# One decoder layer on Trainium2: the gate and up products of both FFNs by a seven-product block scheme

## Chip, cores and metric

One core of one Trainium2 chip runs the whole program. The metric is device time in microseconds (us) for one execution; lower is better.

## What is computed

One inference step of a decoder layer for 1024 prompt tokens and 64 sample tokens, 1088 together, with width 1024 and FFN width 2816, in fp32:

```python
x = x + 0.5 * (silu(h @ w1_gate) * (h @ w1_up)) @ w1_down     # h = rmsnorm(x), first FFN
z = rmsnorm(x) @ w_in                                         # mLSTM q,k,v,i,f,o; attention q,k,v; two gates
y_m = mlstm(z) @ w_up_m
y_a = dilated_attention(z) @ w_up_a
x = x + (sigmoid(gm) * y_m + sigmoid(ga) * y_a) @ w_out
x = x + 0.5 * (silu(h @ w2_gate) * (h @ w2_up)) @ w2_down     # h = rmsnorm(x), second FFN
y = rmsnorm(x)
```

## The kernel before

Everything that is multiplied is split into two float32r parts, a rounded one (hi) and what is left (lo); a product is three matmuls, hi*hi, hi*lo and lo*hi, added in PSUM. Activations lie with features on the 128 partitions and tokens along the free axis; `x` holds [128, 8, 1088] in SBUF. Tokens are cut into three chunks of 384, 384 and 320 (`CHUNKS`).

Weights come as slabs of 128 x 2048 (1 MB) in the order of use. SP loads them into three buffers `raw` (`slab_behind`), GpSimd splits each into `whi` and `wlo` (`split`, L711 and L716, eight pieces of 256 columns each), and TensorE reads them.

An FFN is 11 passes (`step` inside `ffn` of the tensor block), each over 256 hidden columns with three slabs. Slab 1 and 2 hold the gate and up columns of 128 hidden units each. `pair_unit` (L838, L841, L842) makes for one slab and one chunk 8 k x 2 (gate, up) x 3 = 48 matmuls into two PSUM banks. Then ScalarE takes silu of the gate (L1288), VectorE multiplies by up in PSUM (L1731), ScalarE rounds (L1290) and VectorE makes the low part (L1733) into `act_hi`, `act_lo`. `down` (`products`, L811, L814, L815) multiplies slab 3 by these: per chunk eight output tiles of 6 matmuls, through four PSUM banks, and VectorE adds each with factor 0.5 to `x` (L1722). Gate, up and down of a pass stand one after the other in TensorE's order, so only 256 hidden columns exist at a time and `x` stays where it is.

The norm ahead of a product works by chunk: ScalarE squares (L1261), VectorE adds up (L1672), TensorE sums over partitions with a matrix of ones (L822), ScalarE takes the root, VectorE the reciprocal (L1678) and the scaled `htmp` (L1692), ScalarE rounds it to `h_hi` (L1278) and VectorE makes `h_lo` (L1700). At an FFN's end the next norm of chunk 0 lies beside the products of chunk 2 in the last pass.

Behind the first FFN come the value products (45 units of 24 matmuls, 256 wide, L811 with `whi` moving), the other projections (`pair_unit` again), then mLSTM and attention, then the branch products and gates (`mx_hi`, L2201 to L2207) and the output products (`OUNITS`), all in chunks. Every engine's order is written out by hand with semaphores.

## Time and profile before

| | |
|---|---|
| median of 3 runs | 2791.04 us (2786.9 to 2793.04) |
| the profiled execution | 2801.94 us, its span 2799.6 us |
| TensorE busy | 2601.7 us, 16124 matmuls |
| VectorE, ScalarE, GpSimd busy | 949.6, 392.7, 1089.1 us |
| read from memory, written | 172.83 MB, 45.89 MB |

The profiled execution is one of its own, 0.4% above the median. Matmuls are pipelined: their listed durations overlap, and the pace is the distance between starts.

### The profile page before, as it was taken

Reading aid. Unit: us, or ns where it says so; the run is one execution under the profiler, and the core shown is the slowest. Engines: PE = TensorE matmul, PEld = TensorE weight load, DVE = VectorE, ACT = ScalarE, POOL = GpSimd, SP = SyncE. Lnnn points to the kernel's source line nnn. Section 1 sums busy time; section 2 is a strip of 40 time slices with the busy share of each in tenths; the row PEclk is TensorE's granted clock in tenths of the full one; section 3 lists DMA queues with packets and bytes.
Section 4 is the critical chain, followed back from the end, with each engine's and each line's share of the span. In section 5 each row is a group of like instructions: output and inputs, shape, how many; then the busy total and the mean of one; then the engine's idle time right before and its main releaser. Section 6 shows DMA issues by size and latency. Waiting matters only on the chain. (4 is left out here: it accounts for less than half of the span.)

```text
span 2799.6 us, 41223 instructions
## 1 busy us (share of the span) xinstructions
PE 2601.7 (93%) x16124; PEld 2545.1 (91%) x16126; DVE 949.6 (34%) x1885; ACT 392.7 (14%) x823; POOL 1089.1 (39%) x1681
## 2 busy tenths in 40 slices
PE   5899999999989999999996884679899999999997
PEld 5899999999988999999995673679899999999997
DVE  6322222222256101232004575543622222222226
ACT  4100000000022011000113451112200000000003
POOL 5444444444443644343411222232544444444440
PEclk9999999999999999999997897789999999999998
DMA  4111111111101522222315638351111111111101
GB/s 156 46 46 45 45 40 36 44 45 45 45 31 61 171 103 94 93 90 95 94 48 171 210 132 294 133 177 42 46 46 45 45 45 45 45 45 45 45 0 64
DMA packets 85204, 220.24 MB, mean 79 GB/s; under 512 B 10932, under 2 KB 63596, under 8 KB 70124
## 3 DMA queue, kind: packets, MB, share of 16 engines
q1 hardware_dynamic: 60472, 189.25, 19.8%
q10 hardware_dynamic: 24628, 29.50, 3.0%
q8 instruction: 78, 1.28, 0.2%
q14 instruction: 26, 0.21, 0.0%
HBM read 172.83 MB, written 45.89 MB: 78 GB/s over the span
## 5 line engine op out<-in xcount | busy, mean ns | idle before, releaser
L838 PE MATMUL ps<-h_hi,whi 128*128 128x384 f32 (+1 forms) x3072 | 1012.5, 330 | 25.1 <-POOL wlo L716 15.8
L711 POOL TENSOR_TENSOR whi<-raw,con 128x256 fp32r<-128x256 f32 x792 | 474.2, 635 | 1414.3 <-PE ps L838 1119.3
L842 PE MATMUL ps<-h_hi,wlo 128*128 128x384 f32 (+1 forms) x3072 | 1009.2, 329 | 0.7 <-issue 0.7
L841 PE MATMUL ps<-h_lo,whi 128*128 128x384 f32 (+1 forms) x3072 | 1009.2, 329 | 0.0
L838 PEld LDWEIGHTS ps<-h_hi,whi 128*128 128x128 f32 x3072 | 578.1, 188 | 30.9 <-POOL wlo L716 17.9
L841 PEld LDWEIGHTS ps<-h_lo,whi 128*128 128x128 f32 x3072 | 578.3, 188 | 0.6
L842 PEld LDWEIGHTS ps<-h_hi,wlo 128*128 128x128 f32 x3072 | 578.1, 188 | 0.0
L716 POOL TENSOR_TENSOR wlo<-raw,whi 128x256 fp32r<-128x256 f32 x792 | 571.9, 758 | 0.0
L811 PE MATMUL ps<-act_hi,whi 128*128 128x384 f32 (+1 forms) x1056 | 348.3, 330 | 14.4 <-DVE x L1722 14.4
L1731 DVE TENSOR_TENSOR ps<-silu,ps 128x384 f32<-128x384 f32 x132 | 71.3, 540 | 833.3 <-PE ps L842 549.4
L814 PE MATMUL ps<-act_lo,whi 128*128 128x384 f32 (+1 forms) x1056 | 347.4, 329 | 0.0
L815 PE MATMUL ps<-act_hi,wlo 128*128 128x384 f32 (+1 forms) x1056 | 347.1, 329 | 0.0
L1722 DVE SCALAR_TENSOR_TENSOR x<-ps,x 128x384 f32<-128x384 f32 (+1 forms) x528 | 279.3, 533 | 183.8 <-PE ps L815 182.3
L1288 ACT ACTIVATE silu<-ps 128x384 f32<-128x384 f32 x132 | 62.5, 473 | 1260.3 <-PE ps L842 1260.3
L811 PEld LDWEIGHTS ps<-act_hi,whi 128*128 128x128 f32 x1056 | 199.6, 189 | 15.3 <-DVE x L1722 15.1
L814 PEld LDWEIGHTS ps<-act_lo,whi 128*128 128x128 f32 x1056 | 199.5, 189 | 0.3
L815 PEld LDWEIGHTS ps<-act_hi,wlo 128*128 128x128 f32 x1056 | 199.5, 189 | 0.0
L811 PE MATMUL ps<-whi,h_hi 128*128 128x256 f32 x360 | 100.8, 280 | 3.8 <-DVE x L1722 3.8
L815 PE MATMUL ps<-whi,h_lo 128*128 128x256 f32 x360 | 100.4, 279 | 0.0
L814 PE MATMUL ps<-wlo,h_hi 128*128 128x256 f32 x360 | 100.3, 279 | 0.0
L1733 DVE TENSOR_TENSOR act_lo<-ps,act_hi 128x384 fp32r<-128x384 f32 x132 | 70.7, 535 | 71.2 <-ACT act_hi L1290 71.2
L811 PE MATMUL ps<-h_hi,whi 128*128 128x384 f32 (+1 forms) x216 | 72.5, 336 | 12.7 <-POOL wlo L716 10.3
(222 smaller groups left out, 2120.0 us busy)
## 6 DMA issues: line engine op xcount, KB each, us to landing
raw<-stream SPq DMA_DIRECT2D x99, 1024.0 KB, 4.9
vc<-vc_in SPq DMA_DIRECT2D x8, 1170.0 KB, 7.8
kc<-kc_in SPq DMA_DIRECT2D x8, 1152.0 KB, 11.3
zgate<-stage ACTq DMA_DIRECT2D x16, 384.0 KB, 2.5
sgate<-zgate SPq DMA_DIRECT2D x16, 384.0 KB, 3.5
zqko<-stage ACTq DMA_DIRECT2D x12, 384.0 KB, 2.5
oc<-o_att SPq DMA_DIRECT2D x8, 396.0 KB, 6.0
va_out<-sva ACTq DMA_DIRECT2D x24, 130.0 KB, 2.0
```

Of the source, the lines that this page charges most:

```text
L711: pool.tensor_tensor(whi[:, j, cut], raw[:, j, cut], con[:, C_ONES:C_ONES + 1].to_broadcast([P, SPLIT]), ALU.mult).then_inc(hi_split, 1)
L716: low_part = pool.tensor_tensor(wlo[:, j, cut], raw[:, j, cut], whi[:, j, cut].bitcast(F32), ALU.subtract)
L811: mm = pe.matmul(out, w_hi, x_hi, start=(k == 0), stop=False)
L814: pe.matmul(out, w_hi, x_lo, start=False, stop=False)
L815: last = pe.matmul(out, w_lo, x_hi, start=False, stop=(k == nk - 1))
L838: mm = pe.matmul(out, w_hi, h_hi[:, k, a:a + w], start=(k == 0), stop=False)
L841: pe.matmul(out, w_hi, h_lo[:, k, a:a + w], start=False, stop=False)
L842: mm = pe.matmul(out, w_lo, h_hi[:, k, a:a + w], start=False, stop=(k == KT - 1))
L1288: act.activation(silu[:, j, 0:w], bank(2 * j, w), ACT.Silu).then_inc(silu_done, 1)
L1722: dve.scalar_tensor_tensor(x[:, d, a:a + w], bank(4 + v % 4, w), 0.5, x[:, d, a:a + w], ALU.mult, ALU.add).then_inc(acc_free, 1)
L1731: dve.tensor_tensor(up, silu[:, j, 0:w], up, ALU.mult).then_inc(mul_done, 1)
L1733: dve.tensor_tensor(act_lo[:, j, a:a + w], up, act_hi[:, j, a:a + w].bitcast(F32), ALU.subtract).then_inc(pair_free, 1)
```

## The change

The gate and up products become a phase of their own, ahead of all down products. Weights of a gate slab are a 2 x 2 block matrix (gate and up columns; two halves of the 1024 features), and so are the normed tokens (two halves of the features; two blocks of 272 tokens); the 8 block products of their product are made by 7, Winograd's form of Strassen's scheme. The steps:

- Tokens are cut into 2 halves of 544, each into 2 blocks of 272. VectorE's `prepare` scales `x` in place and makes the sums and differences of blocks there; ScalarE's `token_high` rounds the seven operands into `chi`, VectorE writes low parts into `clo` and into `xlo`, which lies where `x` lies. After that `x` itself is gone; it comes back from memory (`x_reload`, the input or a copy stored in `x_kept`) for the down phase.
- A slab's seven weight operands: ScalarE rounds (`gate_high`, 512 columns each), GpSimd makes low parts (`low`) and the four differences in place (`less`). Gate slabs have two buffers.
- `fast` makes for a slab and a token half seven products of 4 k x 3 matmuls, 272 wide, into four PSUM banks; two units alternate between banks 0 to 3 and 4 to 7. VectorE's nine `gate_part` steps combine them, ScalarE takes silu, and the finished 128 x 544 block goes to memory (`hidden_out`) by `gate_store`.
- The down phase loads 256 hidden columns per pass back (`load_hidden`), splits them (`hidden_high`, `hidden_low`) and multiplies as before, in chunks of 384, 384, 320.
- At the FFN's end the norm of chunk 0 begins with the second down chunk. The branch and output products go over four parts of 272 tokens instead of the three chunks. Some semaphores are merged.

```diff
+QW = 272
+PARTS = tuple((QW * i, QW) for i in range(TOK // QW))
+NP = len(PARTS)
+GU = 2 * FFN_ITERS
+FU = 2 * GU
...
+WINO = ((0, 9, 1), (1, 16, 6), (2, 17, 4), (3, 18, 5), (0, 14, 3), (1, 19, 2), (2, 10, 7))
+FSUM_BANK = (0, 4, 0, 4)
...
+        xlo = place("xlo", [P, KT, TOK], F32R, 16512)
...
+            def gate_behind(n, s, b):
+
+                sp.wait_ge(wcl_done, 7 * (s + GU * n - 1))
+                gate_slab(n, s, b)
+
+            def gate_store(n, u, s, q):
+                sp.wait_ge(wino_step, 9 * (u + FU * n) + 9)
+                sp.dma_start(hidden_out[s, :, 2 * QW * q:2 * QW * (q + 1)],
+                             gout[:].rearrange("p j t -> p (j t)")).then_inc(hidden_st, 16)
+
+            def x_reload(n, q):
+                a = slice(2 * QW * q, 2 * QW * (q + 1))
+                sp.dma_start(x[:, :, a], (xT if n == 0 else x_kept)[:, :, a]).then_inc(x_in[1 + q], 16)
+
+            def load_hidden(n, i):
+                sp.wait_ge(hidden_st, 16 * (FU * n + (FU - 2 if i < FFN_ITERS - 1 else FU)))
+                if i > 2:
+                    sp.wait_ge(actlo_done, 3 * (FFN_ITERS * n + i - 2))
+                j = (S_D[n] + i) % 3
+                sp.dma_start(hst[:, j], hidden_out[2 * i:2 * i + 2].rearrange("s p t -> p s t")).then_inc(hst_in[j], 16)
+
...
+                gate_store(n, 41, 20, 1)
+                gate_store(n, 42, 21, 0)
+                x_reload(n, 0)
+                load_hidden(n, 0)
+                gate_store(n, 43, 21, 1)
+                sp.wait_ge(wino_full, 7 * FU * (n + 1))
+                x_reload(n, 1)
+                slab(S_D[n] + 1, (S_D[n] + 1) % 3, shift)
+                load_hidden(n, 1)
+                slab(S_D[n] + 2, (S_D[n] + 2) % 3, shift)
+                for i in range(2, FFN_ITERS):
+                    s = S_D[n] + i + 1
+                    if n == 0 or s < S_D[n] + FFN_ITERS:
+                        slab_behind(s, s % 3, shift)
+                    load_hidden(n, i)
 
...
+            def gate_split(s, b):
+
+                def low(p, col, need):
+                    pool.wait_ge(wch_done, 7 * s + need)
+                    for a in range(0, 512, SPLIT):
+                        cut = slice(a, a + SPLIT)
+                        ins = pool.tensor_tensor(wcl[b][p][:, cut], raw[:, b, col + a:col + a + SPLIT],
+                                                 wch[b][p][:, cut].bitcast(F32), ALU.subtract)
+                    ins.then_inc(wcl_done, 1)
+
+                def less(out, one, two):
+                    for a in range(0, 512, SPLIT):
+                        piece = lambda col: raw[:, b, col + a:col + a + SPLIT]
+                        ins = pool.tensor_tensor(piece(out), piece(one), piece(two), ALU.subtract)
+                    ins.then_inc(wsum_done, 1)
+
+                low(0, 0, 1)
+                low(5, 1536, 2)
+                low(4, 512, 3)
+                less(0, 1024, 0)
+                less(1024, 1536, 1024)
+                pool.wait_ge(wsum_done, 4 * s + 1)
+                less(1536, 1536, 0)
+                low(2, 0, 4)
+                low(3, 1024, 5)
+                low(1, 1536, 6)
+                pool.wait_ge(wsum_done, 4 * s + 3)
+                less(512, 512, 1536)
+                low(6, 512, 7)
...
+            def half_sum_products(f):
+                for k in range(KT):
+                    pe.wait_ge(fsq_ready, 8 * f + k + 1)
+                    for i in range(2):
+                        mm = pe.matmul(bank(FSUM_BANK[f] + i, QW), ones, fsq[:, k % 2, QW * i:QW * (i + 1)],
+                                       start=(k == 0), stop=(k == KT - 1))
+                    mm.then_inc(fsq_used, 1)
+                pe.wait_ge(fsq_used, KT)
...
+            def fast(u, par, b, q, weights=None, tokens_=None, middle=None):
+
+
+                for p, (off, need_h, need_w) in enumerate(WINO):
+                    if p == 0 and not (isinstance(u, int) and u < 2):
+                        pe.wait_ge(wino_step, 9 * u - 10)
+                    if p == 4:
+                        pe.wait_ge(gate_silu, 3 * u + 1)
+                    if p > 4:
+                        pe.wait_ge(wino_step, 9 * u + (p - 4))
+                    if weights is not None:
+                        pe.wait_ge(wcl_done, 7 * weights + need_w)
+                    if tokens_ is not None:
+                        pe.wait_ge(xprep, 19 * tokens_ + need_h)
+                    out = bank(4 * par + off, QW)
+                    lo = low_half(q, p)
+                    for k in range(4):
+                        cut = slice(k * P, (k + 1) * P)
+                        pe.matmul(out, wch[b][p][:, cut], chi[q][p][:, k, :], start=(k == 0), stop=False)
+                        pe.matmul(out, wch[b][p][:, cut], lo[:, k, :], start=False, stop=False)
+                        mm = pe.matmul(out, wcl[b][p][:, cut], chi[q][p][:, k, :], start=False, stop=(k == 3))
+                    mm.then_inc(wino_full, 1)
+                    if p == 0 and middle is not None:
...
+                U, X = FU * n, GU * n
+                b0, b1 = n, 1 - n
+                if n == 0:
+                    half_sum_products(1)
+                fast(U, 0, b0, 0, X, 2 * n, (lambda: half_sum(3)) if n == 1 else None)
+                pe.wait_ge(fstd_ready, 2 * n + 2)
+                fast(U + 1, 1, b1, 0, X + 1)
...
+            def gate_high(s, b, count, kinds):
+
+                for p, col, need in kinds:
+                    if need == 0:
+                        act.wait_ge(graw_in[b], count)
+                    else:
+                        act.wait_ge(wsum_done, 4 * s + need)
+                    act.activation(wch[b][p][:], raw[:, b, col:col + 512], ACT.Copy).then_inc(wch_done, 1)
+
+            PLAIN = ((0, 0, 0), (5, 1536, 0), (4, 512, 0))
+            SUMS = ((2, 0, 1), (3, 1024, 2), (1, 1536, 3))
+            LAST = ((6, 512, 4),)
...
+                    half_square(1, 0)
+                    half_square(1, 1)
+                    token_high(0, 1)
+                    token_high(0, 2)
+                    half_square(1, 2)
+                    half_square(1, 3)
+                    token_high(0, 3)
+                    token_high(0, 4)
+                    token_high(0, 5)
+                    first_slab(0, SUMS)
+                    half_square(1, 4)
+                    half_square(1, 5)
+                    token_high(0, 6)
+                    half_square(1, 6)
+                    half_square(1, 7)
+                half_root(f1)
+                gate_silus(U, 0, 0)
+                first_slab(n, LAST)
+                gate_high(X + 1, b1, loaded + 16, PLAIN)
+                gate_silus(U, 0, 1)
+                token_high(f1, 0)
+                gate_high(X + 1, b1, loaded + 16, SUMS)
+                gate_silus(U, 0, 2)
+                gate_silus(U + 1, 1, 0)
+                token_high(f1, 1)
+                token_high(f1, 2)
+                gate_high(X + 1, b1, loaded + 16, LAST)
+                token_high(f1, 3)
...
+                def slab_time(s, count, b):
+
+
+                    gate_silus(2 * s + U, 0, 0)
+                    act.wait_ge(wino_full, 14 * s + 7 * U)
+                    gate_high(s + (X + 1), b, count, PLAIN)
+                    gate_silus(2 * s + U, 0, 1)
+                    gate_high(s + (X + 1), b, count, SUMS)
+                    gate_silus(2 * s + U, 0, 2)
+                    gate_silus(2 * s + (U + 1), 1, 0)
+                    gate_high(s + (X + 1), b, count, LAST)
+                    gate_silus(2 * s + (U + 1), 1, 1)
+                    gate_silus(2 * s + (U + 1), 1, 2)
...
+                at_ = lambda tile, part: tile[:, part[0], part[1]]
+                if m < 8:
+                    if f >= 2 and m == 0:
+                        dve.wait_ge(x_saved2[q], 16)
+                    tok = slice(2 * QW * q, 2 * QW * (q + 1))
+                    o = C_G + 16 * (f // 2) + m
+                    ins = dve.scalar_tensor_tensor(x[:, m, tok], x[:, m, tok], con[:, o:o + 1], fsum[:, q, :], ALU.mult, ALU.mult)
+                elif m in (10, 11, 12, 14):
+                    dve.wait_ge(xprep, 19 * f + (8, 8, 11, 0, 13)[m - 10])
+                    out, one, two, op = {10: (A22, A21, A22, ALU.add), 11: (A21, A11, A21, ALU.subtract),
+                                         12: (A11, A22, A11, ALU.subtract), 14: (A12, A12, A11, ALU.subtract)}[m]
+                    ins = dve.tensor_tensor(at_(x, out), at_(x, one), at_(x, two), op)
+                else:
+                    part, p, keep, need = {8: (A11, 0, 0, 1), 9: (A22, 6, 2, 2), 13: (A12, 4, 1, 3), 15: (A11, 1, None, 6),
+                                           16: (A22, 2, None, 4), 17: (A21, 3, None, 5), 18: (A12, 5, None, 7)}[m]
+                    dve.wait_ge(xhi_done, 7 * f + need)
+                    dst = at_(xlo, part) if keep is None else clo[q][keep][:]
+                    ins = dve.tensor_tensor(dst, at_(x, part), chi[q][p][:].bitcast(F32), ALU.subtract)
+                ins.then_inc(xprep, 1)
...
+            def gate_part(u, par, m):
+
+                A, B, C, E = (bank(4 * par + i, QW) for i in range(4))
+                S, U4, Y1, Y2 = gsum[:, 0, :], gsum[:, 1, :], gout[:, 0, :], gout[:, 1, :]
...
+                if m == 5 and not (isinstance(u, int) and u == 0):
+                    dve.wait_ge(hidden_st, 16 * u)
...
+                out, one, two = ((S, B, G1), (U4, C, S), (gup[:], E, U4), (S, E, S), (G1, A, G1),
+                                 (Y1, B, U4), (Y1, G1, Y1), (G2, C, S), (Y2, G2, gup[:]))[m]
+                dve.tensor_tensor(out, one, two, ALU.mult if m in (6, 8) else ALU.add).then_inc(wino_step, 1)
...
+                dve.wait_ge(x_in[1], 32 * (n + 1))
+                dve.wait_ge(x_in[2], 32 * (n + 1))
+                downs(0, (S_D[n] + 1) % 3)
...
                 for d in range(KT):
                     accumulate(i, 1, d)
                     if d > 1:
                         add_square(g1 + 1, d - 1)
+                    if d == 4:
+                        inverse(g1)
+                    if d >= 5:
+                        norm_step(g1, d - 5)
...
```

GpSimd, a gate slab. Before, the rows of one slab begin so (`whi`, `wlo`: rounded and low part):

```order
7 L719 ISA
8 L708 ISA
9 L711 ISA
10 L711 TENSOR_TENSOR whi<-raw,con 128x256 x8
11 L715 ISA
12 L716 TENSOR_TENSOR wlo<-raw,whi 128x256
```

Now, the middle of one slab (`wch`, `wcl`: rounded and low operand of a product; `raw<-raw`: a difference of weight blocks):

```order
14 L850 TENSOR_TENSOR raw<-raw 128x256 x4
15 L858 ISA
16 L850 TENSOR_TENSOR raw<-raw 128x256 x2
17 L840 REGISTER_ALU
18 L843 TENSOR_TENSOR wcl_2_110<-raw,wch_2_96 128x256 x2
19 L840 REGISTER_ALU
20 L843 TENSOR_TENSOR wcl_3_111<-raw,wch_3_97 128x256 x2
21 L840 REGISTER_ALU
22 L843 TENSOR_TENSOR wcl_1_109<-raw,wch_1_95 128x256 x2
23 L863 REGISTER_ALU
24 L850 TENSOR_TENSOR raw<-raw 128x256 x2
```

The rounding went to ScalarE; GpSimd has 22 subtractions in place of 8 products and 8 subtractions, and most follow a rounding of ScalarE's.

ScalarE, the head of the program. Before (squares of chunk 0, root, eight roundings, and only then the squares of chunk 1):

```order
1 L1261 ACT_TABLE_LOAD
2 L1261 ACTIVATE ssum<-x 128x384
3 L1261 ACTIVATE sq<-x 128x384 x7
4 L1271 ACT_TABLE_LOAD
5 L1271 ACTIVATE rstd<-ps,con 128x384
6 L1278 ACTIVATE h_hi<-htmp 128x384 x8
7 L1261 ACTIVATE ssum<-x 128x384
8 L1261 ACTIVATE sq<-x 128x384 x7
```

Now, its second part (`chi`: rounded token operands of the first half; `fsq`: squares of the second half; `fsum<-ps`: the second half's root):

```order
14 L1513 ACTIVATE chi_2_82<-x 128x1088
15 L1513 ACTIVATE chi_3_83<-x 128x1088
16 L1513 ACTIVATE chi_1_81<-x 128x1088
17 L1522 ACTIVATE wch_2_96<-raw 128x512
18 L1522 ACTIVATE wch_3_97<-raw 128x512
19 L1522 ACTIVATE wch_1_95<-raw 128x512
20 L1496 ACTIVATE fsq<-x 128x544 x2
21 L1513 ACTIVATE chi_5_85<-x 128x1088
22 L1496 ACTIVATE fsq<-x 128x544 x2
23 L1502 ACTIVATE fsum<-ps,con 128x544
```

The last squares of the second half stand behind the copy `chi_5`, and TensorE's sums over all eight squares (`half_sum_products`) stand ahead of its first product.

SP, from the gate phase to the down phase (before, SP only loads slabs there, each behind `slab_ready`):

```order
35 L510 DMA hidden_out<-gout 128x544 [waits wino_step] x2
36 L515 DMA x<-xT 128x8x544
37 L522 DMA hst<-hidden_out 128x2x1088 [waits hidden_st]
38 L510 DMA hidden_out<-gout 128x544 [waits wino_step]
39 L515 DMA x<-xT 128x8x544 [waits wino_full]
40 L493 DMA raw<-stream 128x2048
41 L522 DMA hst<-hidden_out 128x2x1088 [waits hidden_st]
42 L493 DMA raw<-stream 128x2048
```

The second half of `x` is requested when the last product of the phase has ended.

## Rows read from the trace of the kernel before

**Rows 1.** The page: span, and busy time of each engine

```profile
span 2799.6 us, 41223 instructions
PE 2601.7 (93%) x16124; PEld 2545.1 (91%) x16126; DVE 949.6 (34%) x1885; ACT 392.7 (14%) x823; POOL 1089.1 (39%) x1681
```

**Rows 2.** Stages: stretch, length, busy us (count) PE, PEld, DVE, ACT, POOL, clock, DMA, GB/s

```profile
0.00:23.90 23.90, 1.62 (x2) 0.50 (x2) 12.41 (x15) 8.68 (x14) 12.79 (x21) 1.00 0.88 324
23.90:87.50 63.60, 49.43 (x235) 46.95 (x236) 48.30 (x73) 29.21 (x52) 25.92 (x33) 0.89 0.14 50
87.50:826.30 738.80, 738.80 (x4452) 738.53 (x4451) 208.25 (x383) 66.34 (x137) 315.43 (x492) 1.00 0.12 43
826.30:847.80 21.50, 14.44 (x76) 13.77 (x74) 16.89 (x30) 11.31 (x21) 16.67 (x21) 0.84 0.27 98
847.80:992.50 144.70, 138.51 (x1156) 137.41 (x1155) 50.64 (x92) 9.73 (x21) 65.73 (x96) 0.99 0.36 117
1774.50:1866.60 92.10, 81.00 (x432) 79.40 (x432) 52.87 (x105) 15.53 (x35) 0.00 (x0) 0.89 0.56 187
1877.20:1976.20 99.00, 98.99 (x580) 98.42 (x580) 45.01 (x70) 19.81 (x39) 44.64 (x63) 0.97 0.12 43
2779.20:2799.60 20.40, 1.55 (x3) 0.50 (x2) 15.82 (x27) 2.41 (x5) 0.00 (x0) 0.62 0.39 141
```

**Rows 3.** TensorE in order of time: start, duration, matmul; first and last of three runs

```profile
299.74 0.34 PE L815 MATMUL ps<-act_hi,wlo 128*128 128x384 f32 x1
303.98 0.34 PE L815 MATMUL ps<-act_hi,wlo 128*128 128x384 f32 x1
304.68 0.31 PE L838 MATMUL ps<-h_hi,whi 128*128 128x320 f32 x1
310.84 0.31 PE L838 MATMUL ps<-h_hi,whi 128*128 128x320 f32 x1
929.78 0.28 PE L814 MATMUL ps<-wlo,h_hi 128*128 128x256 f32 x1
931.93 0.28 PE L815 MATMUL ps<-whi,h_lo 128*128 128x256 f32 x1
```

**Rows 4.** GpSimd in order of time: start, duration of eight; FFN 1, then the head

```profile
326.81 5.61 POOL L716 TENSOR_TENSOR wlo<-raw,whi 128x256 fp32r<-128x256 f32 x8
...
30.96 8.10 POOL L716 TENSOR_TENSOR wlo<-raw,whi 128x256 fp32r<-128x256 f32 x8
```

**Rows 5.** Groups by line and shape: busy us, mean ns of one, idle before

```profile
L1731 DVE TENSOR_TENSOR ps<-silu,ps 128x384 f32<-128x384 f32 x88 | 49.5, 562 | 588.7 <-PE ps L842 549.4 <-ACT silu L1288 39.4
L1278 ACT ACTIVATE h_hi<-htmp 128x384 fp32r<-128x384 f32 x48 | 25.1, 522 | 37.3 <-DVE htmp L1692 37.1
L1731 DVE TENSOR_TENSOR ps<-silu,ps 128x320 f32<-128x320 f32 x44 | 21.8, 496 | 244.5 <-ACT silu L1288 244.5
L1678 DVE RECIPROCAL rstd<-rstd 128x384 f32<-128x384 f32 x8 | 20.4, 2553 | 19.1 <-ACT rstd L1271 19.1
L1678 DVE RECIPROCAL rstd<-rstd 128x320 f32<-128x320 f32 x4 | 8.6, 2152 | 5.9 <-ACT rstd L1271 5.9
```

**Rows 6.** VectorE, SBUF to SBUF: beside GpSimd's splits, then (last two) alone

```profile
821.14 0.85 DVE L1692 SCALAR_TENSOR_TENSOR htmp<-x,con,rstd 128x384 f32<-128x384 f32 x1
821.92 0.96 DVE L1700 TENSOR_TENSOR h_lo<-htmp,h_hi 128x384 fp32r<-128x384 f32 x1
...
2766.95 0.55 DVE L1672 TENSOR_TENSOR ssum<-ssum,sq 128x384 f32<-128x384 f32 x1
...
L1692 DVE SCALAR_TENSOR_TENSOR yst<-x,con,rstd x24: 546/609/619, 2756.0 to 2796.6; 128x384 f32<-128x384 f32 x16, 128x320 f32<-128x320 f32 x8
```

**Rows 7.** A load and a store (page), and DMA by slices of 0.75 us, 0 to 30

```profile
raw<-stream SPq DMA_DIRECT2D x99, 1024.0 KB, 4.9
...
zgate<-stage ACTq DMA_DIRECT2D x16, 384.0 KB, 2.5
...
GB/s 0 0 105 197 229 371 399 377 395 476 407 426 366 363 383 379 375 374 371 361 364 364 393 409 425 415 426 448 404 306 33 0 0 109 218 426 371 273 0 0
```

875 lines of the change are left out of this document (543 added, 332 removed).

## Prediction

> **What bounds the kernel now.** I read the page's busy table first, then the table by stages, then the order of time on the single engines. TensorE is busy 2601.7 of 2799.6 us [rows 1], and the chain that ended last is made of it; but a busy share of matmuls says little, so the question is at what pace it goes where, and where it stands. The stages [rows 2] answer: the long stretch of FFN 1 (87.5 to 826.3) is without a hole, at granted clock 1.00, with VectorE at 28%, ScalarE at 9%, GpSimd at 43% and DMA at 12%. TensorE's own pace sets the end there, and only fewer or narrower matmuls help. Between them lie short stages in which norms, weight splits and loads stand in its way.
>
> That pace is read from starts of consecutive matmuls [rows 3]: 128x384 goes from 299.74 to 303.98 in 24 steps, 0.1767 us each; 128x320 from 304.68 to 310.84 in 42, 0.1467 us; 128x256 from 929.78 to 931.93 in 19, 0.1132 us. Their listed durations (about 0.3 us) are latencies and overlap. One pass over 256 hidden columns has 288 of the wide and 144 of the narrow matmuls, a third of each in the down products: 50.9 + 21.1 = 72.0 us. Eleven passes are 792 us. FFN 1 ends at 847.8, so it loses 55.8 us, 46.9 at its head (23.9 before the first product) and 8.9 at its end, where 76 matmuls, some 12.6 us, fill 21.5; FFN 2 runs from 1976.2 to 2779.2 and loses 11.
>
> **What the change removes.** A gate slab (128 gate and 128 up columns) has 144 matmuls now: 96 x 0.1767 + 48 x 0.1467 = 24.0 us. The new scheme has 2 token halves x 7 products x 4 k x 3 split terms = 168 matmuls of 272 columns. No row has that width. By the straight line from 256 to 320 one takes 0.1216 us; by the 256-wide price per column 0.1203; by the line through 320 and 384 carried down 0.1242. I take 0.122, near the first, and keep 0.120 and 0.1245. A slab is then 168 x 0.122 = 20.5 us, 3.5 less; 44 slabs give **-154 us**. At the two ends it is -169 and -136. The down products keep their 144 matmuls: 24.0 us a pass.
>
> **Does another engine set the pace of the gate phase?** Each against 20.5 us a slab.
> - GpSimd: 14 subtractions for low parts and 8 for weight differences, all 256 wide, two operands. Eight now start 5.6 us apart in all, 0.70 each [rows 4]: 22 x 0.70 = 15.4, plus about 1 us of waiting for ScalarE's rounded copies. It can begin a slab only when TensorE starts the slab before: ScalarE's first copy stands behind its read of that slab's first product, some 2.3 us in. It ends about 19 us in, so some 4 us are spare.
> - ScalarE: 7 copies 512 wide and 6 steps 272 wide; at 522 ns for 384 [rows 5], no more than 7 x 0.70 + 6 x 0.52 = 8.0 us.
> - VectorE: 18 parts 272 wide; 562 ns at 384, 496 at 320 [rows 5] make 0.45: 8.1 us.
> - PSUM: product 5 overwrites bank 0 after ScalarE copied it out (due 5.9 us in, done by 2.5), and banks change sides between units; nothing is late. Stores of 278 KB and loads of 1 MB per 20.5 us are some 80 GB/s, against 324 moved in the first 23.9 us [rows 2].
> - SP: behind its wait for a slab's last low part (about 19 us into the slab before) stands the store of that slab's second unit, due at 21; VectorE's 6th part of the next unit waits for that store, due near 29. A store of 384 KB lands after 2.5 us [rows 7], so nothing stops.
>
> So TensorE still sets the pace. GpSimd is the one with little room. Where VectorE adds or scales from SBUF to SBUF meanwhile, the same eight subtractions took 8.10 us, and VectorE's 384-wide steps 0.96 us instead of 0.55 [rows 4, 6]; beside VectorE operations with a PSUM operand they took 5.6. In the steady phase 4 of 18 parts have no PSUM operand, 1.6 us a slab, and by the rows the cost is within the spare 4 us. The Trainium skill (SBUF — State Buffer, the shared port pair) says that a VectorE operation with two SBUF inputs and a GpSimd operation exclude each other for a whole instruction, which speaks against this change; by that rule GpSimd would need 15.4 + 1.6 + 1 = 18 us here, still under 20.5, and the contended rows agree with it.
>
> **What the change adds, at the joins.**
> - Head of FFN 1. TensorE now waits for half of all tokens and, before its first product, for the square sums of the other half; ScalarE's last two squares stand behind a copy that needs VectorE's 15th preparation step. The walk: x rows land at about 10 us, adds to 16, sum and root to 18.6, reciprocal 3.6 (2553 ns at 384, 2152 at 320 [rows 5]) to 22.2, eight scalings 544 wide to 28 and seven steps 1088 wide to 37 (609 ns at 384 and 546 at 320 [rows 6] carry on to 0.76 and 1.3), copies, weight copies, squares and sums to 42. The first unit then ends at about 55, since the clock is low after idling (0.89 over the first stage after the start now [rows 2]). Slab 1's copies stand behind silu and preparation: 7 us of stall; the second half's preparation, partly at contended prices, another 6 to 9; slab 2's split can start only when the third unit has left its buffer, 2 us. Head in all about 64 instead of 46.9: **+17** (bounds +8, all preparation at free prices, to +30, all at contended ones).
> - Gate to down, twice. x was used up as combinations and comes back from memory; its second half, 2.23 MB, is requested when the last product ends. A 1 MB load lands after 4.9 us alone [rows 7], so 10.7 at that rate, 5.6 at the about 400 GB/s that the first window's best slices reach [rows 7]; I take 8. VectorE waits for it, and TensorE runs four products (4.2 us) ahead into its four banks. Stall some 6, with the clock 8: **+16** for both (8 to 30). The split of the first down slab is hidden behind the last two units.
> - End of FFN 1. The norm of chunk 0 no longer lies beside gate products of chunk 2 but inside the last 15.5 us of down products: VectorE has 2.55 of reciprocal, 16 accumulations, 16 square additions and 8 steps at about 1.9 (0.85 and 0.96 [rows 6]) there, about 31 us; chunk 1's norm slides into the value products. Together 26 us lost against 8.9 + 10.3 (144.7 us for 134.4 of products after it): **+7** (0 to 15).
> - Mixer outputs in four parts of 272: 576 + 768 matmuls at 0.122, 164 us, for 168 now. The out products take 99.0 us now [rows 2], and gain about 4; the branches (92.1 for 72 of products [rows 2]) hang on VectorE and the gate loads, 32 rounds instead of 24, and lose about 3. **-1** (-5 to 8).
> - Head of FFN 2. First slab's weight differences come after the last out product, 5 us; then the same stalls as above, about 18: 23 for 11 now. **+12** (5 to 22).
> - Tail. The last chunks' norms meet a VectorE that also accumulates; from the start of the second down chunk (now 15.5 us ahead of 2779.2 [rows 2]) the root comes at 8, the reciprocal at 10.4, chunk 1's sum at 17, the last product at 23, the last square's addition at 35, scaled outputs and stores at 45; 36 now. **+9** (5 to 12).
>
> Attention between 1473 and 1774 keeps its work. Sum: -154 + 17 + 16 + 7 - 1 + 12 + 9 = -94 against 2801.94 us, the profiled execution's own time, 0.4% over the median 2791.04. So 2707 for a profiled one and, by the same 0.4%, **2697 us** as median.
>
> **Rivals.**
> - *GpSimd sets the pace* (slower). If its 22 operations cost what eight cost beside VectorE's SBUF work, 8.10/8 = 1.01 us [rows 4], a slab takes 22 x 1.01 + 0.8 = 23.0 us, and 44 x 2.5 = 110 us come back: 2807, slower. It eats the whole gain from 0.99 us per operation on; at 0.93 the loss is 33 us (2730). For it: 15.4 of 20.5 us in use, two operands throughout, chains to ScalarE. Against: 0.70 in the steady phase [rows 4]. 12 in 100, 5 of them past the turning point.
> - *Narrow matmuls cost their columns alone*: 272 at 2.4 GHz are 0.1133 us. Then 44 x 168 x 0.0087 = 64 us more, 2633. For it: what a row adds to its columns falls with the width, 16.7 ns at 384 and 6.5 at 256 [rows 3]. Against: no row is without it. 6 in 100. The Trainium skill (TensorE: Matmul & The Clock Gate, Back-to-back issue gap) adds a fixed 2.5 ns to the columns; by that rule the result would be 2651, but every interval of this trace is longer than it gives.
> - *The joins cost all that they can*: 117 instead of 60, 2754. 10 in 100.
> - *It doesn't do what it says*: if a slab still issued 192 matmuls of 272, it would take 23.4 us and gain 27 us, less than the joins cost. The order of instructions has seven products of 12 per half; 1 in 100.
>
> **How the numbers follow.** The forecast has 71 in 100. Its own bounds: joins at their low sum of 21 and a matmul at 0.120 give 2643; joins at 117 and 0.1245 give 2772. I let the range end at 2645 and 2765, which takes in the milder GpSimd cases and leaves out the cheap matmuls and the worst corners. A measurement here tells 0.2%, 5.6 us, from no change. Faster 0.92, same 0.02, slower 0.06 (GpSimd past its turning point, and 1 for what I don't see).
>
> **What would show it.** In the new profile: gate matmuls 0.120 to 0.1245 us apart at clock 1.00; 168 per 20.5 us; GpSimd's pairs about 1.4 us with idle time before each slab; a start at about 42 us; a hole of 5 to 8 us between gate and down; some 31 us for the last two down chunks of FFN 1. TensorE waiting for low weight parts all through the gate phase, or intervals over 0.13, would prove me wrong.

## The result, and the profile after

The changed kernel takes 2781.15 us (median of 6 runs, 2771.38 to 2785.04) against 2793.14 (6 runs, 2786.9 to 2805.1): ratio 0.9943 with a 95% interval of [0.992, 0.9967] (the medians alone divide to 0.9957). It is faster, as forecast, but by some 0.5% for the forecast 3.4%; 2781 lies above the range. The profiled execution took 2771.38 us, its span 30.1 us less than before [rows 1]. It is the fastest of the six, and the profiled execution of the kernel before lies 9 us above its median, so the stages account for 30 us of gain where the medians show 12. All stage figures below are of that execution, unless a run is named. Below, a *unit* is the 84 gate products of one weight slab and one half of the tokens, two units to a slab; the *head* of an FFN is the time up to about its sixth unit, from which on TensorE hardly waits in the gate phase (the *steady run*); the *join* is where the gate phase ends and the first down pass begins; the *tail* is the end of the program.

The page of the changed kernel, the lines that answer to [rows 1]:

```profile
span 2769.5 us, 47348 instructions
PE 2514.5 (91%) x17550; PEld 2452.1 (89%) x17550; DVE 1261.0 (46%) x2482; ACT 593.7 (21%) x1165; POOL 1348.7 (49%) x1945
```

Its stages, columns as in [rows 2]: in FFN 1 the start, the head, the steady run, the join (hole and first down pass) and the last down pass; then the branch, the out products, and the head of FFN 2:

```profile
0.00:44.00 44.00, 14.14 (x37) 9.57 (x37) 27.46 (x26) 23.77 (x33) 16.59 (x24) 0.96 0.39 152
44.00:133.97 89.97, 70.26 (x504) 69.41 (x505) 51.73 (x74) 28.04 (x48) 56.25 (x69) 0.87 0.15 52
133.97:502.90 368.93, 368.93 (x2943) 368.93 (x2942) 148.14 (x315) 111.85 (x229) 276.21 (x386) 1.00 0.20 75
536.20:572.60 36.40, 27.29 (x146) 26.83 (x145) 17.49 (x30) 4.33 (x6) 19.22 (x29) 0.91 0.76 297
787.10:821.55 34.45, 28.34 (x151) 26.19 (x149) 30.25 (x54) 15.78 (x30) 13.42 (x16) 0.90 0.08 31
1745.50:1850.10 104.60, 83.93 (x575) 82.23 (x576) 58.42 (x143) 18.05 (x49) 0.00 (x0) 0.88 0.55 170
1860.80:1960.00 99.20, 99.20 (x771) 99.04 (x772) 43.30 (x63) 20.82 (x27) 33.53 (x52) 0.98 0.15 55
1960.00:2064.20 104.20, 74.85 (x512) 73.24 (x511) 57.00 (x75) 30.56 (x52) 63.52 (x85) 0.84 0.19 70
```

The third line is the phase that the change was made for: 35 units of 84 products in 368.93 us, TensorE without a hole at clock 1.00, so 368.93 / 2940 = 0.1255 us a product and 21.08 us a slab. The lines around it are where that gain went: heads at clock 0.84 to 0.87 with 22% and 28% of TensorE's time empty, a join with 27 of 36 us busy, a branch that grew from 92.1 [rows 2] to 104.6.

GpSimd in the middle of the steady run, one slab (start, duration, form, idle before), beside [rows 4]; last, eight of its subtractions in the head:

```profile
347.61 4.21 POOL L843 TENSOR_TENSOR wcl<-raw,wch 128x256 fp32r<-128x256 f32 x6 [4.55 <-ACT wch L1522]
351.77 4.42 POOL L850 TENSOR_TENSOR raw<-raw 128x256 f32<-128x256 f32 x6
356.16 4.42 POOL L843 TENSOR_TENSOR wcl<-raw,wch 128x256 fp32r<-128x256 f32 x6
360.54 1.43 POOL L850 TENSOR_TENSOR raw<-raw 128x256 f32<-128x256 f32 x2
362.70 1.43 POOL L843 TENSOR_TENSOR wcl<-raw,wch 128x256 fp32r<-128x256 f32 x2 [0.74 <-ACT wch L1522]
...
46.76 7.70 POOL L843 TENSOR_TENSOR wcl<-raw,wch 128x256 fp32r<-128x256 f32 x8 [2.12 <-ACT wch L1522]
```

From 347.61 to 364.13 it does its 22 operations, with 4.55 us idle before them: the spare 4 us of the prediction. In the head eight take 7.70 us, near the 8.10 of [rows 4].

By the prediction's own terms, in us, from the two profiled spans (a slab before is 24.0 us, a down pass 72.0 / 3):

| term | forecast | measured | how |
|---|---|---|---|
| gate slabs | -154 | -128.5 | 44 x (24.0 - 21.08) |
| head of FFN 1 | +17 | +25.4 | last gate product at 536.1, less 22 x 21.08 = 463.8, less 46.9 |
| two joins | +16 | +26.4 | hole 4.7 and first pass 31.8 for 23.8; 4.6 and 32.9 for 23.8 |
| end of FFN 1 | +7 | -1.9 | last pass 34.3, value stage 141.2 for 134.4 of products; 19.2 lost before |
| branch and out | -1 | +12.8 | 104.6 for 92.1, 99.2 for 99.0, 0.1 between |
| head of FFN 2 | +12 | +31.6 | 506.3 from the last out to the last gate product, less 463.8, less 10.9 |
| tail | +9 | +7.2 | last pass 31.5 for 23.8, 0.5 less behind it |
| rest | 0 | -3 | down passes 23.8 for 24.0; projections, attention +1 |
| sum | -94 | -30 | |

### The profile page after: what moved, and what is told of

It is laid out like the page before. It is cut to its first block and busy times, and to the rows that moved or that the text cites. A ratio compares the mean times of both kernels' runs of the same rounds, so it can differ in the third digit from the quotient of the medians.

```text
span 2769.5 us, 47348 instructions
## 1 busy us (share of the span) xinstructions
PE 2514.5 (91%) x17550; PEld 2452.1 (89%) x17550; DVE 1261.0 (46%) x2482; ACT 593.7 (21%) x1165; POOL 1348.7 (49%) x1945
## 5 line engine op out<-in xcount | busy, mean ns | idle before, releaser
L1054 PE MATMUL ps<-chi,wch 128*128 128x272 f32 x2464 | 718.9, 292 | 50.7 <-POOL wcl L843 34.0
L1056 PE MATMUL ps<-chi,wcl 128*128 128x272 f32 x2464 | 717.5, 291 | 0.0
L843 POOL TENSOR_TENSOR wcl<-raw,wch 128x256 fp32r<-128x256 f32 x616 | 450.7, 764 | 350.1 <-ACT wch L1522 350.1
L1054 PEld LDWEIGHTS ps<-chi,wch 128*128 128x128 f32 x2464 | 471.2, 191 | 53.7 <-POOL wcl L843 36.0
L1056 PEld LDWEIGHTS ps<-chi,wcl 128*128 128x128 f32 x2464 | 470.4, 191 | 0.0
L1055 PE MATMUL ps<-xlo,wch 128*128 128x272 f32 x1408 | 411.1, 292 | 0.0
L979 PE MATMUL ps<-act_hi,wsp 128*128 128x384 f32 (+1 forms) x1056 | 353.2, 334 | 23.6 <-DVE x L2132 14.8
L982 PE MATMUL ps<-act_lo,wsp 128*128 128x384 f32 (+1 forms) x1056 | 350.0, 331 | 0.0
L983 PE MATMUL ps<-act_hi,wsp 128*128 128x384 f32 (+1 forms) x1056 | 349.7, 331 | 0.0
L1006 PE MATMUL ps<-h_hi,wsp 128*128 128x384 f32 (+1 forms) x960 | 314.6, 328 | 2.9 <-issue 1.8
L1010 PE MATMUL ps<-h_hi,wsp 128*128 128x384 f32 (+1 forms) x960 | 314.2, 327 | 0.0
L979 PEld LDWEIGHTS ps<-act_hi,wsp 128*128 128x128 f32 x1056 | 201.8, 191 | 27.1 <-DVE x L2132 16.8
L983 PEld LDWEIGHTS ps<-act_hi,wsp 128*128 128x128 f32 x1056 | 201.9, 191 | 0.0
```

The costliest lines, as they stand in the source:

```text
L843: ins = pool.tensor_tensor(wcl[b][p][:, cut], raw[:, b, col + a:col + a + SPLIT], wch[b][p][:, cut].bitcast(F32), ALU.subtract)
L979: mm = pe.matmul(out, w_hi, x_hi, start=(k == 0), stop=False)
L982: pe.matmul(out, w_hi, x_lo, start=False, stop=False)
L983: last = pe.matmul(out, w_lo, x_hi, start=False, stop=(k == nk - 1))
L1006: mm = pe.matmul(out, w_hi, h_hi[:, k, a:a + w], start=(k == 0), stop=False)
L1010: mm = pe.matmul(out, w_lo, h_hi[:, k, a:a + w], start=False, stop=(k == KT - 1))
```

## Experiments

The edits are shortened to what matters; words in brackets and `...` stand for code left out.

### The pace of a product by its width

Edit: the program is replaced. It leaves out the layer and runs products by TensorE alone, then with neighbours.

```diff
+stretch(across(512)); stretch(across(128)); stretch(across(256)); ...
+stretch(values(old_hi[0], old_lo[0])); stretch(values(old_hi[0], old_hi[1]))
```

> A kernel of its own that leaves out the whole computation: TensorE alone runs stretches of 768 float32r products (each with its weight load, in triples hi-hi, hi-lo, lo-hi as in the kernel), 128 to 512 columns wide, then the 256-wide pattern of the value products with the high and low weights 24 KB and 8 KB apart, then 272 columns from an address 16 bytes on, then 272 with GpSimd, VectorE, ScalarE and all three copying beside it. Theory 'the width itself': 272 columns take 0.1255 us with nothing beside them, as in the changed kernel, and the other widths lie where they were (0.113 to 0.1175 at 256, 0.1466 at 320, 0.176 at 384); the neighbours change nothing. Rival 'neighbours': 272 alone takes the 0.122 that the straight line between 256 and 320 gives, and 0.125 or more only with the other engines beside it. Rival 'distance of the operands': the 256-wide pattern takes 0.113 us with the parts 24 KB apart and 0.1175 with 8 KB.

Stretches of 768 products, columns as above: 128, 256, 272, 320, 384 columns wide; the pattern of the value products with the two weight parts 24 and 8 KB apart; 272 with all engines beside it:

```profile
220.10:306.20 86.10, 85.95 (x768) 85.83 (x768) 0.00 (x0) 0.00 (x0) 0.00 (x0) 1.00 0.00 0
306.30:397.10 90.80, 90.69 (x768) 90.52 (x768) 0.00 (x0) 0.00 (x0) 0.00 (x0) 1.00 0.00 0
491.00:587.20 96.20, 96.03 (x768) 95.84 (x768) 0.00 (x0) 0.00 (x0) 0.00 (x0) 1.00 0.00 0
689.80:802.80 113.00, 112.88 (x768) 112.64 (x768) 0.00 (x0) 0.00 (x0) 0.00 (x0) 1.00 0.00 0
803.00:936.40 133.40, 133.37 (x768) 133.07 (x768) 0.00 (x0) 0.00 (x0) 0.00 (x0) 1.00 0.00 0
1116.30:1207.00 90.70, 90.62 (x768) 90.52 (x768) 0.00 (x0) 0.00 (x0) 0.00 (x0) 1.00 0.00 0
1207.00:1298.10 91.10, 90.77 (x769) 90.52 (x768) 0.00 (x0) 0.00 (x0) 0.00 (x0) 1.00 0.00 0
1780.00:1876.50 96.50, 96.13 (x769) 95.87 (x768) 96.29 (x109) 46.22 (x150) 96.25 (x108) 1.00 0.00 0
```

From first to last start a product takes 0.1117 us at 128 columns, 0.1179 at 256, 0.1215 at 264, 0.1248 at 272, 0.1329 at 288, 0.1468 at 320, 0.1734 at 384. The width alone makes 0.1248 of the 0.1255; neighbours change nothing (0.1249), the distance of the parts nothing (0.1179 both), and 16 bytes of offset add 0.0006. From 128 to 256 columns the price hardly rises: 128 cost 95% of 256.

The straight line from 256 to 320 that the prediction drew holds in this stream: it gives 0.1251 at 272. What does not hold is the price at its lower end, 0.1132 [rows 3], which this stream does not reach (0.1179). The trace of the kernel before has both prices, in one stage. These two products stand 138 steps apart, so 0.1178 us a step:

```profile
882.80 0.28 PE L814 MATMUL ps<-wlo,h_hi 128*128 128x256 f32 x1
899.05 0.28 PE L814 MATMUL ps<-wlo,h_hi 128*128 128x256 f32 x1
```

Behind them come 24 products 320 wide, and from 902.8 to 992.5 us the same value products take 0.1133. The clock is 1.00 in both stretches, and GpSimd is idle in the first and busy for 50.9 of 89.6 us in the second. In the changed kernel both stretches of this stage run at 0.1178. What sets the pace over was not found.

### Two pieces of the change alone

```diff
-whi = place("whi", [P, 3, SLAB], F32R); wlo = ...
+wsp = place("wsp", [P, 3, 2, SLAB], F32R); whi = [wsp[:, (j + 2) % 3, 0, :] ...]; wlo = ...
...
-for c, (a, w) in enumerate(CHUNKS):   (branch: loads, splits, products, gates)
+for c, (a, w) in enumerate(PARTS):
```

> The kernel before, with two pieces of the change alone: high and low weights side by side per slab, as after, and the mixer's branch in four parts of 272 columns (the out products stay in three chunks). Theory 'the pieces cost what the changed kernel shows': the 256-wide value products go from 0.1133 to 0.1175 us and the value stage from 144.7 to 149 us; the stretch from the branch's first product to the first out product goes from 102.7 to 113 to 115 us, so the whole is 15 to 18 us slower. Rival 'layout costs nothing': value products stay at 0.1133. Rival 'rounds cost nothing': the branch stays within 3 us of 102.7, and the longer branch after comes from its loads or from the memory around it.

Value stage and branch:

```profile
854.50:990.90 136.40, 133.98 (x1132) 133.41 (x1131) 42.34 (x82) 7.31 (x16) 60.53 (x90) 0.99 0.38 124
1769.70:1872.50 102.80, 84.06 (x576) 81.96 (x576) 58.35 (x143) 18.05 (x49) 0.00 (x0) 0.89 0.52 162
```

The layout costs nothing: the value products run as in the kernel before, at 0.1178 up to 897.6 us and at 0.1133 from 901.2 on, and take 136.3 us from first to last (137.2 in the kernel before). In the changed kernel they take 135.9 although all run at 0.1178: that price costs 3.6 us on the last 791 of them, and shorter holes at the stage's start make it up. The parts cost what the changed kernel shows: 102.8 us for 92.1, and 2805.56 us for 2792.22 of the kernel before, single runs. The branch's loss is its own, 32 rounds (one output tile each) for 24 and one boundary between parts more, and no work of the FFNs around it.

### The loads' places in the branch

```diff
-if c + 1 < NP and d >= 2: load_branch(c + 1, d - 2)   (branch_high, branch_low alike)
+if c + 1 < NP and d < 6: load_branch(c + 1, d)
...
-if n == 2: sp.dma_start(x[:, 0:XB], x_kept[:, 0:XB])
+if 2 <= n < 2 + XB: sp.dma_start(x[:, n - 2], x_kept[:, n - 2])
```

> The changed kernel with other places for the loads in the mixer's branch: the next part's inputs are loaded and split in rounds 0 to 5 of a part instead of 2 to 7, and the first rows of x come back one row a round instead of in one transfer. The 32 rounds take 3.16 us in the mean, 2.2 to 2.6 where nothing is late; three part boundaries take 5.3 to 5.8, the round behind the return of x 9.6. Theory 'more rounds and more boundaries': each boundary loses 2 to 3 us, the round behind the return 5 to 7, and the branch goes from 104.6 to 88 to 93 us. Rival 'bytes': the loads only move and delay other rounds, the branch stays over 100 us.

The branch's window of this kernel, and TensorE's waits in that of the changed kernel (waited for: us in total, times, longest):

```profile
1746.10:1832.20 86.10, 78.81 (x576) 75.95 (x576) 57.33 (x143) 18.06 (x49) 0.00 (x0) 0.96 0.66 206
```

```profile
PE ps L979 <- DVE mh_lo L2645: 11.9, 3, 6.8
PE ps L979 <- DVE mx_lo L2607: 10.4, 4, 3.6
```

86.1 us for 104.6, better than expected. By VectorE's first step of a round, the rounds over a boundary fell from 5.3 to 5.8 us to 2.1, the round behind the return of x from 9.6 to 3.2. TensorE's wait for the next part's low halves (`mx_lo`) fell from 10.4 to 1.7 us and that for the low parts behind the late gate loads (`mh_lo`) from 11.9 to 7.2: both hung on the order of a queue, for the same bytes moved. The whole took 2758.59 us in a single run. The first down pass of its second FFN took 41.3 us for 32.9 in the changed kernel; one low part of the hidden units, a VectorE operation with both operands in SBUF, lasted 7.54 us there. The next experiment shows such a wait.

### The order at the joins

```diff
-x_reload(n, 0); load_hidden(n, 0); gate_store(n, 43, 21, 1); sp.wait_ge(wino_full, ...); x_reload(n, 1)
+load_hidden(n, 0); x_reload(n, 0); sp.wait_ge(wino_full, ...); x_reload(n, 1); gate_store(n, 43, 21, 1)
...
-for m in range(7): gate_part(last, m); hidden_low(0, 0); gate_part(last, 7); gate_part(last, 8); hidden_low(0, 1); ...
+for m in range(9): gate_part(last, m); for c in range(NC): hidden_low(0, c)
...
-dve.wait_ge(x_in[1], ...); dve.wait_ge(x_in[2], ...); downs(0)
+for c: dve.wait_ge(x_in[1 + c], ...) if c < 2; accumulate(0, c, 0..7); hidden_low(1, c)
```

> The changed kernel with another order at the two joins from gate to down products: the first hidden units are loaded ahead of the first half of x, the second half of x is asked for ahead of the last store, VectorE finishes the last gate unit before it takes the low part of the hidden units, and waits for the second half of x only at the second chunk. Theory 'order of the queues': the first down pass goes from 31.8 and 32.9 us to 25 to 27, the waits around it from 12.6 and 13.6 to 4 to 6 each, the kernel by 14 to 18 us down. Rival 'the bytes': 5.5 MB have to pass at the join in any order, and the waits stay at 10 us or more each, the gain under 6 us.

TensorE's waits at the first join, changed kernel (536 to 573), then this one (548 to 582):

```profile
PE ps L979 <- DVE x L2132: 4.7, 1, 4.7
PE ps L979 <- DVE act_lo L2138: 4.4, 1, 4.4
```

```profile
PE ps L979 <- DVE x L2130: 3.1, 1, 3.1
PE ps L979 <- DVE act_lo L2136: 2.7, 1, 2.7
```

Holes and longer first passes cost 9.5 and 7.5 us (3.0 + 6.5, 3.0 + 4.5) for 12.7 and 13.7: 9.4 us back, between the two expectations. So more than a third of the joins was order; the wait for the low part of the hidden units (2.7 us: last gate step, ScalarE's copy, VectorE's difference) stays. All the same the kernel took 2782.75 us, in a single run. The reason lay elsewhere, and is the finding of this study. The gate phase of its first FFN has seven holes of 1.7 to 1.8 us and that of its second six, where the changed kernel's profiled execution has one each (both have one more of 1.3 us in the second head). VectorE and GpSimd at one of them:

```profile
144.70 0.44 DVE L2116 TENSOR_TENSOR gout<-ps,gsum 128x272 f32<-128x272 f32 x1 [1.15 <-PE ps L1056]
145.27 7.22 DVE L2116 TENSOR_TENSOR gout<-gsil,gout 128x272 f32<-128x272 f32 x1
152.41 0.43 DVE L2116 TENSOR_TENSOR gsil<-ps,gsum 128x272 f32<-128x272 f32 x1
```

```profile
142.35 4.27 POOL L850 TENSOR_TENSOR raw<-raw 128x256 f32<-128x256 f32 x6
146.53 4.28 POOL L843 TENSOR_TENSOR wcl<-raw,wch 128x256 fp32r<-128x256 f32 x6
150.69 1.50 POOL L850 TENSOR_TENSOR raw<-raw 128x256 f32<-128x256 f32 x2
154.18 1.44 POOL L843 TENSOR_TENSOR wcl<-raw,wch 128x256 fp32r<-128x256 f32 x2 [1.99 <-ACT wch L1522]
```

A product of VectorE with both factors in SBUF takes 7.22 us for 0.44. It ends at 152.49, just after GpSimd's unbroken row does (152.19); its neighbours with a factor in PSUM take 0.43 and 0.44, the one ahead of it beside the same row. Behind it stand ScalarE's next silu and copy out of PSUM, and TensorE, which may overwrite that bank only then, stops from 151.81 to 153.64.

### The two products out of the way

```diff
-(gup, E, U4), (S, E, S), (G1, A, G1), (Y1, B, U4), (Y1, G1, Y1), (G2, C, S), (Y2, G2, gup)
+(S, E, S), (E, E, U4), (G1, A, G1), (B, B, U4), (Y1, G1, B), (G2, C, S), (Y2, G2, E)
...
-pe.wait_ge(wino_step, 9 * u - 10)
+pe.wait_ge(wino_step, 9 * u - 9)
```

> The changed kernel, where VectorE's two products of a gate unit take one factor from PSUM and no longer both from SBUF (two sums stay in their banks; the two steps before them change places, and the bank is given back one step later). In the three looks at the changed kernel and its variants 3, 16 and 11 of the 88 first products took 2.6 to 7.2 us for 0.44 to 0.9, each while GpSimd's row of 128x256 differences ran without a hole, and each of 7 us held TensorE for 1.8 us, in other slabs in every run. Theory 'two SBUF operands wait until GpSimd pauses': no product over 1 us is left, no stall of 1.8 us inside the gate phases is left, the runs lie within 4 us of each other and their median at 2764 to 2771 us, against 2781 with a spread of 14 for the changed kernel. Rival 'the stall has another cause' (the store of the unit before, the loads' places in SyncE's queue): the products of 7 us stay or pass to another step, the median stays at 2778 to 2784.

The groups (busy us, mean ns, idle before) of the changed kernel, of the one with the other joins, and of this one:

```profile
L2118 DVE TENSOR_TENSOR gout<-gsil,gout 128x272 f32<-128x272 f32 x88 | 76.5, 869 | 10.8 <-DVE gout L2118 0.5
```

```profile
L2116 DVE TENSOR_TENSOR gout<-gsil,gout 128x272 f32<-128x272 f32 x88 | 150.3, 1708 | 10.8 <-DVE gout L2116 0.5
```

```profile
L2118 DVE TENSOR_TENSOR gout<-gsil,ps 128x272 f32<-128x272 f32 x176 | 77.1, 438 | 83.3 <-ACT gsil L1547 35.9 <-PE ps L1056 33.2 <-DVE ps L2118 2.2
```

All 176 products now take 436 to 440 ns, and no hole is left in the steady run; the gate phases take 488.7 and 498.8 us, against 492.1 and 506.1 in the changed kernel's profile and 503.0 and 515.4 in that of the other joins. Timed: 2759.21 us (2748.44 to 2772.39, 4 runs), ratio to the kernel before 0.9877 [0.983, 0.9924], for 0.9943 [0.992, 0.9967]: better, though the intervals just touch, and 5 us better than expected. That the products were held by GpSimd's row, and that a factor in PSUM frees them, is shown by the groups. That the whole gain is theirs is not: the branch, whose code is the same, took 97.3 us for 104.6 in this profile, and the three held products of the changed kernel's profile made holes of only 4.8 us together (14 made 24.9 in that of the other joins). The expected small spread is not there either (24 us; the kernel before, beside it, 21), so other things vary from run to run too.

### The heads

```diff
-half_root(0); token_high(0, 0); half_square(1, 0); half_square(1, 1); token_high(0, 1); ... first_slab(0, SUMS); ...
+half_root(0); half_square(1, 0..7); half_root(1); first_slab(0, SUMS); token_high(0, 0..3); first_slab(0, LAST); gate_high(1, PLAIN); ...
...
-gate_silus(U, 0, 1); token_high(f1, 0); gate_high(X + 1, SUMS)
+gate_high(X + 1, SUMS[0:2]); gate_silus(U, 0, 1); gate_high(X + 1, SUMS[2:3]); token_high(f1, 0)
```

> The changed kernel with another order on ScalarE at the two heads: in FFN 1 the squares of the second half and the sums' high parts of slab 0 stand in the stretch in which it waited for VectorE (18 to 26 us), and slab 1's high parts ahead of the first tokens of the second half; in FFN 2 only the last of these; slab 2's high parts ahead of a silu. Theory 'ScalarE's order holds the heads': the first gate product comes at 30 to 38 us for 44.0, the stall of 10.9 us before the second unit shrinks to 3 to 6 in both heads, FFN 1's head loses 9 to 13 us of its 72.4, FFN 2's 4 to 6 of its 41. Rival 'GpSimd holds the heads' (about 22 sums and low parts a slab at 0.7 us free and over 1 us beside VectorE's preparation): work that starts earlier only runs more slowly, and the heads lose under 4 us together.

TensorE's waits from 30 to 136 us in the changed kernel, then in this one:

```profile
PE ps L1054 <- POOL wcl L843: 14.1, 2, 10.7
PE ps L1054 <- DVE xlo L2095: 5.6, 2, 4.9
```

```profile
PE ps L1054 <- DVE xlo L2095: 21.4, 3, 10.5
PE ps L1054 <- POOL wcl L843: 7.2, 3, 3.4
PE ps L1054 <- DVE clo L2095: 4.9, 1, 4.9
```

The first gate product comes at 34.6 us for 44.0, as expected, and nothing is won: the sixth unit starts at 123.8 for 123.5. GpSimd's share of the waits halves and VectorE's grows by 20.7 us. In FFN 2, where only slab 1's sums and one silu changed places, the sixth unit starts 85.9 us behind the first for 92.1: 6.2 back. So ScalarE's order held part of that head and nothing of the first. The whole took 2776.65 us in a single run, with nine held products in its profile.

### Whose work fills the first head

```diff
+for again in range(2 if f < 2 and keep is not None else 0):
+    link(dve.tensor_tensor(dst, at_(x, part), chi[q][p][:].bitcast(F32), ALU.subtract))
```

> The changed kernel, where VectorE computes three of the low parts of each half of the tokens of FFN 1 three times instead of once (12 more differences of 128x1088, 1.28 us each alone and 1.82 beside GpSimd: 15 to 22 us of VectorE's time, 6 to 9 before the first products of the gate and the rest behind). In the changed kernel the sixth gate unit, the first of the steady run, starts at 123.5 us. Theory 'VectorE's preparation sets the head': it starts at 138 to 146. Rival 'GpSimd's weight splits set it': only the part ahead of the first units counts, it starts at 124 to 132.

```diff
+if twice: pool.tensor_tensor(wcl[b][p][:, cut], raw[:, b, ...], wch[b][p][:, cut], ALU.subtract)   (first two slabs)
```

> The changed kernel, where GpSimd computes each low part of the first two slabs of FFN 1 twice (28 more differences of 128x256, 0.73 us alone and 0.9 to 1.8 beside VectorE: 20 to 30 us, half of it per slab). Theory 'GpSimd's weight splits set the head': the sixth gate unit starts 18 us or more later than 123.5, at 141 to 155. Rival 'VectorE's preparation sets it': the first unit waits some 5 us longer and the stall of 10.9 us before the second grows, but slab 2's splits stay where the tokens of the second half let them, and the unit starts at 125 to 135.

TensorE's waits from 30 to 136 us with more work on VectorE, then with more on GpSimd:

```profile
PE ps L1054 <- POOL wcl L843: 14.1, 2, 10.7
PE ps L1054 <- DVE xlo L2097: 12.0, 3, 11.0
```

```profile
PE ps L1067 <- POOL wcl L853: 26.3, 3, 21.3
PE ps L1067 <- DVE xlo L2108: 5.7, 2, 4.9
```

Up to the sixth unit VectorE was busy 17.1 us longer (92.2 for 75.1), and the unit starts at 135.8, 12.3 later; GpSimd 23.1 longer (87.5 for 64.3), and the unit starts at 138.9, 15.4 later. Both fall between their two expectations: some 70% of either engine's added work reaches TensorE. Neither sets the head alone; the path passes from one to the other. That less work on either would shorten it was not tried. The whole took 2779.07 and 2810.22 us, in single runs; the second of these holds 19 products of VectorE for 7.1 to 7.2 us, so its length is not the head's alone.

### All together

The edits of the joins, the heads, the branch and the two products in one kernel.

> All together: the products from PSUM, the other order at the joins and at the heads, the other places of the loads in the branch. From the changed kernel's profiled span of 2769.5 us: joins -8 as in their look, head of FFN 2 -7, head of FFN 1 0, branch -12 to -16, the stalls in the gate phases -2 to -20 by the run. If the parts add up, a median of 2733 to 2745 us. If one of them only moves a wait (the earlier branch meets the same loads, the shorter head the same GpSimd), 2750 or more.

Its span, and its branch, the steady gate run of FFN 1 and the first down pass behind it:

```profile
span 2721.7 us, 47356 instructions
```

```profile
1730.80:1813.80 83.00, 78.55 (x576) 75.51 (x576) 57.62 (x143) 18.08 (x49) 0.00 (x0) 0.97 0.68 210
121.20:531.90 410.70, 410.70 (x3276) 410.70 (x3275) 155.23 (x351) 120.99 (x247) 297.50 (x426) 1.00 0.21 79
535.00:560.90 25.90, 25.66 (x145) 25.35 (x146) 15.78 (x28) 2.15 (x3) 16.75 (x25) 0.93 0.92 365
```

2728.34 us (2724.01 to 2735.06, 4 runs), ratio 0.9759 [0.972, 0.9798] to the kernel before: the parts add up and more (2733 to 2745 was expected). It beats both kernels. A product of its steady gate run takes as long as ever, 410.70 / 3276 = 0.1254 us (39 units).

## Why the prediction was wrong

The sign, the bound and the direction of most terms were right. TensorE sets the pace of the gate phase; GpSimd's rival, which the prediction feared most, did not happen; joins and heads take back part of the gain. What failed is sizes, and most of them in the same direction. Together they make the 64 us between -94 and -30; the end of FFN 1, which cost less than forecast, hides 9 us of the misses, by luck.

- **The gate slab (26 us of the 64).** The step that failed is "I take 0.122, near the first" of three ways to 272 columns. It measured 0.1255, above even the bound of 0.1245. The straight line was sound; the price at its lower end was not. "128x256 from 929.78 to 931.93 in 19, 0.1132 us" was read where the value products run at the lower of their two paces; up to 899 us they run at 0.1178 in the same stage, as in the stream of that width alone and in the changed kernel. With 0.1178 the line gives 0.1250 and the term -132, near the measured -128.5. So 22 of the 26 us are that one price. The rival "columns alone" was off by 12.2 ns a product, the forecast by 3.5; its reason, that what a row adds to its columns falls to 6.5 ns at 256, came from the same price (11.1 with 0.1178). The Trainium skill (TensorE: Matmul & The Clock Gate, Back-to-back issue gap) has a fixed 2.5 ns over the columns for a matmul by itself, and says that this falls short where each has a weight load and few columns. The trace of the pace experiment is longer than that figure at each width: 272 columns (0.1133) take 11.5 ns more, 384 (0.160) 13.4.
- **Head of FFN 2 (20 us) and of FFN 1 (8).** The failing step is "then the same stalls as above, about 18", and above it "7 us of stall" before the second unit: that one is 10.9 us in FFN 1 and 10.6 in FFN 2. In FFN 2 the holes come to 31 us for the 23 forecast (6.6, 10.6, 7.2, 3.7 and smaller ones). Behind each of these four 16 to 24 products start 0.23 us apart, for 0.1255 at clock 1.00, at a granted clock of 0.50, which is the lower level of 1.2 GHz: some 10 us of low clock (0.84 over the window 1960.00 to 2064.20), which the prediction counted at the first start and at the joins, but not behind the holes of a head. The runs with added work, on the head of FFN 1, show that VectorE's preparation and GpSimd's splits lie on that path in turns; "partly at contended prices" priced one engine at a time.
- **Branch and out products (14 us).** The failing steps are "and lose about 3" and "gain about 4". The rounds where nothing is late go at TensorE's own pace, 2.24 to 2.26 us for 18 products of 0.1255, so the products of the branch cost 72.3 us for 71.0 in the kernel before (16 rounds of 3.12 and 8 of 2.64), about as priced. The time lost beside them was taken to grow little; it grew from 21 us to 32, at one boundary more and at the round behind the return of x. The pieces alone reproduce it in the kernel before (30), and other places for the loads take 18.5 us off (14 left). The out products gained nothing, 99.2 us for 99.0: 0.1255 for 0.122 is 2.7 us of the missing 4.
- **Joins (10 us).** The forecast priced the transfer of x, "Stall some 6", and that size held (4.2 to 4.7 and the clock). It left out a second wait, the low part of the first hidden units, which VectorE computes in the middle of its last gate unit: another 4.4 to 4.7 at each join. With the other order 9.4 us came back.
- **End of FFN 1 (-9 us, the other way).** The last pass lost 10.5 us, not the 15.5 that "about 31 us" for two chunks implied, and the value stage took up less of the rest.
- **What the prediction didn't see at all.** The step "by the rows the cost is within the spare 4 us" treated VectorE's two SBUF products as a price in GpSimd's time. They hit VectorE instead: most of those that begin beside a GpSimd operation take up to 1.0 us, and now and then one waits until GpSimd pauses, 7 us later, of which 1.8 us reach TensorE in the steady run. The profiled execution has 3 such products, those of the other joins and of the other heads 14 and 9. The changed kernel's median lies 10 us above its profiled time; that such waits are part of this is likely and not shown, since the timed runs have no trace.

## What to carry to other kernels

Price a product of a new width from a stream of that width; and before a pace from twenty products goes into a sum, look in the same trace whether the same product keeps it: 4.6 ns at one end of the line were 22 us of this sum. When a change multiplies the boundaries between phases, price each boundary as a chain over all engines, with every wait in it and the clock after it: here the phase won 128 us, and the boundaries gave 98 back, of which other orders in the queues and the two products from PSUM, together, recovered 48 (profiled spans of 2769.5 and 2721.7 us). Where VectorE has work with two SBUF operands beside a GpSimd that works in unbroken rows, put one operand into PSUM.
